# Two halves of the activations in one product: a block product per bank in the up projection of a decoder block

## What is computed

```python
up = rmsnorm(h, g_ffn) @ w_up                  # 512 x 2048 @ 2048 x 11264
up = causal_depthwise_conv(up, conv_w, conv_b) # width 3
gate, val = jnp.split(up, 2, axis=-1)
h = h + (jax.nn.silu(gate) * val) @ w_down     # 512 x 5632 @ 5632 x 2048
```

## Time and profile before

| | us |
|---|---|
| median of 3 runs | 2804.92 (2804.79 to 2805.13) |
| the profiled execution, its own time | 2804.52 |
| its span in the trace | 2803.0 |
| busy in the span: TensorE, its weight loads | 2796.8, 2512.3 |
| busy in the span: VectorE, ScalarE, POOL | 2086.9, 1249.5, 428.8 |

### The profile page before, as it was taken

How to read it: one execution, slowest core, us unless ns; L and a number is a source line. 1 busy time by engine, 2 the same in 40 slices (tenths; PEclk the granted TensorE clock), 3 DMA queues, 4 the chain that set the end, 5 groups by cost and what they waited for, 6 DMA issues and landing times.

```text
span 2803.0 us, 45334 instructions
## 1 busy us (share of the span) xinstructions
PE 2796.8 (100%) x16930; PEld 2512.3 (90%) x16930; DVE 2086.9 (74%) x3913; ACT 1249.5 (45%) x1701; POOL 428.8 (15%) x579
## 2 busy tenths in 40 slices
PE   9999999999999999999999999999999999999999
PEld 7888888888889998888899999999999999999998
DVE  7776777677678777444468987888788878887884
ACT  5444343443434334333355544444444444444543
POOL 2022144323400000000000111111011101010112
PEclk9999999999999999999999999999999999999999
DMA  5464586665535555444455665566656555565567
GB/s 181 142 177 103 170 203 133 170 189 119 120 111 161 174 167 175 149 134 147 139 175 141 144 139 136 133 138 136 136 136 136 136 136 136 136 137 138 135 136 166
DMA packets 187463, 411.24 MB, mean 147 GB/s; under 512 B 22288, under 2 KB 50320, under 8 KB 186128
## 3 DMA queue, kind: packets, MB, share of 16 engines
q1 hardware_dynamic: 120240, 283.90, 32.5%
q0 software_dynamic: 67040, 124.82, 24.2%
HBM read 347.81 MB, written 112.72 MB: 164 GB/s over the span
## 4 chain that ended last, share of the span: by engine, by line
PE 98%; DVE 1%; ACT 0%; issue 0%; DMA 0%; SPq 0%; DVEq 0%
PE bank L1881 12%; PE bank L1883 12%; PE bank L1882 12%; PE bank L2151 11%; PE bank L2153 11%; PE bank L2152 11%; PE bank L2186 6%; PE bank L2187 6%; PE bank L2188 6%; PE bank L2107 3%; PE bank L2109 3%; PE bank L2108 3%; PE bank L1955 1%; PE bank L1989 1%; PE bank L2000 0%; PE bank L1945 0%
## 5 line engine op out<-in xcount | busy, mean ns | idle before, releaser
L2151 PE MATMUL bank<-v_hi,w_hi 128*128 128x256 f32 x2464 | 697.6, 283 | 0.0
L2153 PE MATMUL bank<-v_hi,w_lo 128*128 128x256 f32 x2464 | 697.3, 283 | 0.0
L2152 PE MATMUL bank<-v_lo,w_hi 128*128 128x256 f32 x2464 | 697.3, 283 | 0.0
L937 ACT ACTIVATE w_hi<-w_raw 128x896 fp32r<-128x896 f32 (+1 forms) x528 | 445.2, 846 | 552.1 <-DVE w_raw L1677 384.5
L1684 DVE TENSOR_TENSOR w_lo<-w_raw,w_hi 128x896 fp32r<-128x896 f32 (+1 forms) x528 | 500.0, 953 | 124.5 <-ACT w_hi L937 123.5
L2151 PEld LDWEIGHTS bank<-v_hi,w_hi 128*128 128x128 f32 x2464 | 472.9, 192 | 2.0 <-issue 0.2
L2152 PEld LDWEIGHTS bank<-v_lo,w_hi 128*128 128x128 f32 x2464 | 472.9, 192 | 1.9 <-issue 0.2
L2153 PEld LDWEIGHTS bank<-v_hi,w_lo 128*128 128x128 f32 x2464 | 472.9, 192 | 0.0
L1881 PE MATMUL bank<-u_hi,w_hi 128*128 128x512 f32 x1000 | 395.4, 395 | 0.2 <-DVE w_lo L1078 0.2
L1883 PE MATMUL bank<-u_hi,w_lo 128*128 128x512 f32 x1000 | 389.9, 390 | 0.0
L1882 PE MATMUL bank<-u_lo,w_hi 128*128 128x512 f32 x1000 | 389.3, 389 | 0.0
(11 more groups left out here) (290 smaller groups left out, 4848.7 us busy)
## 6 DMA issues: line engine op xcount, KB each, us to landing
w_raw<-wslots SPq DMA_DIRECT2D x504, 256.0 KB, 2.7
w_raw<-wstream SPq DMA_DIRECT2D x189, 512.0 KB, 3.6
out_t<-stage POOLq DMA_DIRECT2D x168, 256.0 KB, 4.4
sums_scratch<-wfirst POOLq DMA_DIRECT2D x72, 448.0 KB, 5.8
g_raw<-sums_scratch SPq DMA_DIRECT2D x48, 448.0 KB, 3.3
g_raw<-wgates SPq DMA_DIRECT2D x48, 256.0 KB, 2.8
w_raw<-sums_scratch SPq DMA_DIRECT2D x24, 448.0 KB, 3.3
sums_scratch<-sums_scratch POOLq DMA_DIRECT2D x72, 128.0 KB, 4.6
```

What stands on the lines that cost most here:

```text
L937: act.activation(w4_hi[ring][:, 0:width], w4_raw[ring][:, 0:width], ACT.Copy).then_inc(w4_hi_ready, 1)
L2151: nc.tensor.matmul(out, wh, xh, start=kp == 0 and half == 0, stop=False, skip_group_check=True)
L2152: nc.tensor.matmul(out, wh, xl_, start=False, stop=False, skip_group_check=True)
L2153: ins = nc.tensor.matmul(out, wl, xh, start=False, stop=kp == KP - 1, skip_group_check=True)
```

## The change

For the tiles f = 7 to 43 (`WIDE` = 7) the up slots are computed in another way.

- The high and the low activations of a place lie in one tensor, `v_parts`. High weights times high activations (256 columns) and high weights times low activations (256 columns) become one matmul of 512 columns. It fills a whole bank: the left half with the first, the right half with the second. Low weights times high activations is added to the left half. A slot is 7 matmuls of 512 and 7 of 256 columns.
- The 7 block products take banks 0 to 6. The down outputs of a tile go to banks 7, 0, 1, 7 (d0 to d0 + 3); those behind the last tile go to banks 2 to 5.
- In a slot all high weights come first, behind a wait for the high part alone, and then the low ones, behind a wait for the low part. In the last slot, kp = 7, banks 0 to 2 come first with both parts (`EARLY` = 3), then banks 3 to 6. Down slots also take their high weights first.
- At q = 8 ScalarE copies the right halves of the banks (`low_halves`), three together ahead of its `hi_slot` and four together behind it, in place of the half bank of `p1_copy`; VectorE adds the left halves to them (`add_halves`), in two more instructions, the first ahead of its `sums` and `lo_slot`, the second at the head of `combine`. `bank_free` stands on TensorE ahead of each bank's first product of a tile. `combine_wide` and `take_up_wide` do the same five steps as before, from SBUF.
- `take_down(d0 + 2)` moves from q = 2 of the next tile to q = 11, behind `hi_slot(n + 3)`; `take_down(d0 + 3)` moves from q = 4 to q = 2.

```diff
+WIDE_PRODUCTS = [(A11, B11), (S2, T2), (S3, T3), (A22, T4), (S1, T1), (A12, B21), (S4, B22)]
...
+    def down_bank(d):
+        if d >= END:
+            return bank[2 + d % GROUP]
+        return bank[(7, 0, 1, 7)[d % GROUP] if wide(d // GROUP + 2) else GROUP + d % GROUP]
...
+            def low_halves(f, late):
+                if late:
+                    act.wait_ge(slot_done, START_F[f] + KP)
+                    act.wait_ge(s_raw_ready, f)
+                    act.activation(part_list(late_sum, 4), bank_halves(EARLY, 7, 1),
+                                   ACT.Copy).then_inc(low_copied, 1)
+                else:
+                    act.wait_ge(early_done, f - WIDE + 1)
+                    act.wait_ge(up_out, f - 1)
+                    act.activation(part_list(early_sum, EARLY), bank_halves(0, EARLY, 1),
+                                   ACT.Copy).then_inc(low_copied, 1)
...
-                if f > 2 and q in (2, 4):
+                if 2 < f < WIDE and q in (2, 4):
                     take_down(n, d0 - 2 + (q == 4), slots_done)
+                if f >= WIDE and q == 2:
+                    take_down(n, d0 - 1, slots_done)
...
                     if q == KP + 2:
                         conv_term(n, f, 0)
                         take_down(n, d0 + 1, slots_done)
                     if q == KP + 3:
+                        take_down(n, d0 + 2, slots_done)
                         conv_term(n, f, 1)
...
+            def add_halves(f, late):
+                k = 2 * (f - WIDE) + late
+                sums, j0, j1 = (late_sum, EARLY, 7) if late else (early_sum, 0, EARLY)
+                dve.wait_ge(low_copied, k + 1)
+                dve.tensor_tensor(part_list(sums, j1 - j0), bank_halves(j0, j1, 0), part_list(sums, j1 - j0),
+                                  ALU.add).then_inc(drained, 1)
...
+            def bank_free(f, j):
+                d = GROUP * (f - 3)
+                if f == WIDE:
+                    if j >= GROUP:
+                        pe.wait_ge(down_out, GROUP + d + j - GROUP + 1)
+                    return
+                pe.wait_ge(drained, 2 * (f - WIDE) - (j < EARLY))
+                if j < 2:
+                    pe.wait_ge(down_out, GROUP + d + j + 2)
...
+            def wide_high(f, kp, ring, j):
+                w, x = WIDE_PRODUCTS[j]
+                both = v_parts[kp][:, :].rearrange("p (a c) -> p a c", a=2)[:, :, x * HALF:(x + 1) * HALF]
+                if kp == 0:
+                    bank_free(f, j)
+                nc.tensor.matmul(bank[j].rearrange("p (a c) -> p a c", a=2), w4_hi[ring][:, w * P:(w + 1) * P], both,
+                                 start=kp == 0, stop=False, skip_group_check=True)
```

More of the change, by code:

```diff
@@ L281, in build_program @@
     ntri, nones, nmask = (sb(n, P, tile[j]) for j, n in enumerate(("ntri", "nones", "nmask")))
-    bank = [nc.alloc_psum_tensor(f"bank{j}", [P, SEQ], F32) for j in range(8)]
+    banks = nc.alloc_psum_tensor("bank", [P, 8 * SEQ], F32)
+    bank = [banks[:, j * SEQ:(j + 1) * SEQ] for j in range(8)]
     Z = bank[2:6]
@@ L1008, in position @@
                 slots_done = place(n)[0]
+                if wide(f) and q == KP:
+                    low_halves(f, False)
+                hi_slot(n + 3)
                 d0 = GROUP * (f - 2)
@@ L1045, in position @@
                     if q == KP:
-                        p1_copy(n, f)
+                        if wide(f):
+                            low_halves(f, True)
+                        else:
+                            p1_copy(n, f)
                     if q == KP + 1:
@@ L1706, in _, with combine_wide @@
             lo_slot(1)
+            def add_halves(f, late):
[4 more added lines that the diff above has]
+                                  ALU.add).then_inc(drained, 1)
+            def combine_wide(f):
+                k, done = 2 * (f - WIDE), f * DVE_STEPS4
+                dve.wait_ge(drained, k + 1)
+                dve.tensor_tensor(part(early_sum, 1), part(early_sum, 1), part(early_sum, 0),
+                                  ALU.subtract).then_inc(dve4_step, 1)
+                dve.wait_ge(dve4_step, done + 1)
+                dve.tensor_tensor(part(early_sum, 2), part(early_sum, 1), part(early_sum, 2),
+                                  ALU.subtract).then_inc(dve4_step, 1)
+                dve.wait_ge(drained, k + 2)
+                dve.scalar_tensor_tensor(out=part(early_sum, 3), in0=part(late_sum, 1), scalar=-1.0,
+                                         in1=part(early_sum, 1), op0=ALU.mult, op1=ALU.subtract).then_inc(dve4_step, 1)
@@ new lines, in take_up_wide @@
+            def take_up_wide(f):
+                done = f * DVE_STEPS4
+                dve.wait_ge(dve4_step, done + 2)
+                dve.tensor_tensor(a_pad[1][:, PAD:PAD + SEQ].rearrange("p (a c) -> p a c", a=2),
+                                  part(early_sum, 2).unsqueeze(1).broadcast_to((P, 2, HALF)),
+                                  part_list(late_sum, 2), ALU.add).then_inc(dve4_step, 1)
+                dve.wait_ge(dve4_step, done + 3)
+                first_last = early_sum[:, :].rearrange("p (b c) -> p b c", c=HALF)[:, 0:4:3, :]
+                dve.tensor_tensor(a_pad[0][:, PAD:PAD + SEQ].rearrange("p (a c) -> p a c", a=2),
+                                  late_sum[:, 2 * HALF:4 * HALF].rearrange("p (a c) -> p a c", a=2),
+                                  first_last, ALU.add).then_inc(up_out, 1)
@@ L1722, in take_up @@
             def take_up(n, f):
+                if wide(f):
+                    take_up_wide(f)
+                    return
                 fn = f
@@ L1776, in position @@
             def position(n):
-                sums(n + 3)
-                lo_slot(n + 2)
                 at_ = n
@@ L1782, in position @@
                 q = at_ - START_F[f]
+                if wide(f) and q == KP:
+                    add_halves(f, False)
+                sums(n + 3)
+                lo_slot(n + 2)
                 if at_ == 0:
@@ L2134, in _, with wide_low, wide_products, down_free @@
                 unit3(KP - 1, p, p % 2, p // 2)
+            def bank_free(f, j):
[3 more added lines that the diff above has]
+                        pe.wait_ge(down_out, GROUP + d + j - GROUP + 1)
+                    return
+                pe.wait_ge(drained, 2 * (f - WIDE) - (j < EARLY))
[8 more added lines that the diff above has]
+                                 start=kp == 0, stop=False, skip_group_check=True)
+            def wide_low(kp, ring, j):
+                w, x = WIDE_PRODUCTS[j]
+                return nc.tensor.matmul(bank[j][:, 0:HALF], w4_lo[ring][:, w * P:(w + 1) * P], part(v_hi[kp], x),
+                                        start=False, stop=kp == KP - 1, skip_group_check=True)
+            def wide_products(at_, f, kp, ring):
+                for j0, j1 in ((0, EARLY), (EARLY, 7)) if kp == KP - 1 else ((0, 7),):
+                    for j in range(j0, j1):
+                        wide_high(f, kp, ring, j)
+                    if j0 == 0:
+                        pe.wait_ge(w4_ready, at_ + 1)
+                    for j in range(j0, j1):
+                        ins = wide_low(kp, ring, j)
+                    if j1 == EARLY:
+                        ins.then_inc(early_done, 1)
+                return ins
+            def down_free(d):
+                f, i = d // GROUP + 2, d % GROUP
+                if not wide(f):
+                    pe.wait_ge(down_out, d + 1)
+                elif d >= END + GROUP:
+                    pe.wait_ge(down_out, d + 1)
+                elif d >= END:
+                    pe.wait_ge(drained, 2 * (FT - WIDE))
+                elif i == 0:
+                    pe.wait_ge(down_out, GROUP + d)
+                elif i == 3:
+                    pe.wait_ge(down_out, GROUP + d - 2)
+                else:
+                    pe.wait_ge(drained, 2 * (f - WIDE) + 1)
             def up_slot(n):
@@ L2145, in up_slot @@
                     pe.wait_ge(up_out, (f - 1))
+                if wide(f):
+                    pe.wait_ge(w4_hi_ready, at_ + 1)
+                    wide_products(at_, f, kp, ring).then_inc(slot_done, 1)
+                    return
                 pe.wait_ge(w4_ready, at_ + 1)
@@ L2174, in down_slot @@
                 pe.wait_ge(first_out, 1)
-                pe.wait_ge(w4_ready, at_ + 1)
+                pe.wait_ge(w4_hi_ready, at_ + 1)
                 for c, d, fs, first, last in entry(n)[1]:
                     pe.wait_ge(s_ready, fs[-1] + 1)
-                    pe.wait_ge(down_out, d + 1)
+                    down_free(d)
                     if d == DOWNS[-1][0]:
+                        pe.wait_ge(w4_ready, at_ + 1)
                         ins = in_halves(ring, kk, fs, first)
                         continue
[L2182 to L2189, removed]
+                    out = down_bank(d)[:, :]
+                    for k, f in enumerate(fs, kk):
+                        wh = w4_hi[ring][:, k * P:(k + 1) * P]
```

(7 more changed lines are left out.)

53 lines of the change are left out of this document (32 added, 21 removed).

## The result

The changed kernel takes 2827.17 us (2827.16 to 2827.26), the one before 2804.98 in the runs beside it: the ratio is 1.0079, 95% interval 1.0067 to 1.0091, slower by 22.2 us. The forecast was 2818.0, slower by 13.1, in a range of 2802 to 2834.

A forecast was written before the change was run, and what follows sets the result against it. TensorE's own instructions were taken to set the time. A saving of 27 us, 38.5 us of stalls at 36 boundaries and 1.6 us in the last tile summed to +13.1 us: 2818.0 us, in a range of 2802 to 2834.

The forecast's parts named there:

- its own case: The forecast itself: a stall of 0.87 to 1.3 us a boundary, 2811 to 2826 us; chance 0.64.
- TensorE's saving: Up slots: 7 wide matmuls replace 14 narrow, saving 0.091 us a slot, 0.73 a tile, 27 us in all.
- The stall: TensorE waits for bank 1 at each of 36 tile boundaries: 1.07 us each, bounds 0.9 and 1.5, 38.5 us in all.
- The late copy: ScalarE's copy at a tile's end has 1024 elements, not 256: 0.969 us, later by 0.585.
- In the last tile: The fourth down slot waits for bank 7, which holds d0: 1.6 us, once.
- VectorE's first sums of the next tile: Late copy and late addition shift VectorE's chain by 1.72 us: these sums start at +3.47 instead of +1.75.
- The early part: Copy and addition for banks 0 to 2 end before +0.9, needed at +2.73: hidden, costing nothing.
- The transfer as a second lock: `take_down(d0 + 2)` also waits for d0's transfer, until +11.22 to +11.43, as late as ScalarE; 0.06 us added a boundary.
- rival C: Transfers decide: d0's comes 0.5 us later, stall 1.5 us, 2833.5 us; chance 0.12.
- A: Faster: bank 1 is free in time, the 1.72 us shift swallowed, no boundary stalls, 2778 us; chance 0.10.
- B: About the same: five VectorE chain steps cheaper from SBUF, some 0.3 us together, stall 0.75, 2806.5 us; chance 0.10.
- D: The wide product's moving operand in two runs, 7168 bytes apart, loses the 27 us saving: 2845 us; chance 0.04.

The follow-up runs named there:

- e1: Changed kernel with ScalarE taking d0 + 2 out of bank 1 ahead of the high part of up slot 2, not behind it: 2810.61 us.
- e3: Changed kernel with ScalarE taking d0 + 2 ahead of the high part of up slot 2, into a third stage (early_sum): 2785.22 us.
- e4: Changed kernel with only TensorE's order edited: in a wide tile's first slot banks 2 to 6 come first, banks 0 and 1 last: 2785.44 us.
- e9: Changed kernel with the first slot's products in bank order 0, 2, 3, 1, 4, 5, 6, so bank 1 is wanted two products later: 2810.43 us.
- e5: e4's kernel with each wide product again two matmuls of 256 columns, into the two halves of the same bank: 2809.00 us.
- e6: e4's kernel with high and low activations of a block side by side, so the moving operand is one run of 512: 2785.29 us.

## Why the prediction was right, and by how much it was not

The direction, the place and the mechanism were right; e1, e3, e4 and e9 show each that TensorE loses 36 times the time between wanting bank 1 and getting it. The size was less good: 22.2 us were measured for 13.1, within the range, but 1 us above the 2811 to 2826 that the prediction gave to its own case. Three terms of the sum were off.

- **TensorE's saving**: forecast 27 us (0.73 a tile). Measured 20.15 - 19.55 = 0.60 a tile, 22 us. The rate of the wide product was an average over the 48 of the down stage, most of which come behind their like. In the changed kernel seven follow on seven narrow ones, and take 2212.67 - 2211.06 = 1.61 us, 0.230 each. The kernel before has exactly that price in its trace, 1.62 us for the first seven behind a narrow one; the prediction saw it as a slow start in the average and corrected the wrong way, from 0.088 to 0.091 us a slot, where it was the very place that the new products would have. A slot is 19.55 / 8 = 2.44 us and not the 2.43 of the sum (2.444 and 2.427). That makes 5 us.
- **The stall**: forecast 1.07, measured 31.63 - 30.47 = 1.16 us, a tile less one of e4. The late copy took 1.03 and not 0.97, and TensorE started 0.14 behind the copy's end, where the earlier trace rows had shown 0.05. 36 x 0.09 = 3 us.
- **POOL's late issue** in one tile: 0.6 us, not in the sum. The trace of the kernel before had it, in the same tile.

13.1 + 5 + 3 + 0.6 = 21.7 of the 22.2 us. In the last tile TensorE waited for 1.4 us, about as forecast. All three misses point the same way; twice as large, they would have carried the time out of the range, which ends at +29.

Point by point: VectorE's first sums of the next tile started at +3.53, forecast +3.47. VectorE was busy for 10.62 + 16.79 = 27.4 us of the tile, forecast at most 27.7, and didn't become the bound. The early part hid, as no wait names it. The transfer as a second lock was there (e1, e3), but it opened 0.6 us ahead of ScalarE and not beside it: the turnaround of 4.92 and 5.13 us had been read off two transfers of the last tile, and in the others it is near 4.5 (e1). Why those two took longer isn't shown. Here are POOL's issues of d0 and of d0 + 2 in the changed kernel:

```profile
2202.92 0.85 POOL L662 DMA_DIRECT2D out_t<-stage  x1 [17.50 <-ACT stage L1031]
...
2208.90 0.85 POOL L662 DMA_DIRECT2D out_t<-stage  x1 [0.87 <-ACT stage L1031]
```

With the issue at +6.37 the stage was free at about +10.9, and ScalarE came at +11.48. The 0.06 us added for it were for nothing, and of rival C, slower because transfers decide, only the one late tile came true. The upper bound of 1.06 for the late copy can't be had from the earlier trace rows, which give 1.07 to 1.08; with 1.03 measured it changed nothing.

Of the rivals: A (the shift is swallowed) falls with the chain above, in which VectorE has no gap. B (five VectorE steps cheaper from SBUF) falls too: the steps of `take_up` have 0.60 us each in the chain, from SBUF, and their form of 512 had 0.684 us as duration before and has 0.68 now, so the table of the Trainium skill in "VectorE: DVE Perf Modes" (its section on the TRN2 errata), by which a step from PSUM would be an estimated 65 ns dearer than one from SBUF, is again not what this trace shows. D (the two runs eat up the saving) falls with e5 and e6. By the fixed 2.5 ns that the Trainium skill gives in "TensorE: Matmul & The Clock Gate", section "Wait — 56ns, not 53.3ns?", e5 would have been an estimated 5 us slower than e4; it was 23.6.

## What to carry to other kernels

When two uses share a buffer that each had for itself, write down the date on which it comes free and the date on which it is wanted, through every engine's fixed order; the difference, times the number of times, is the price, and it can exceed what the change saves on the busiest engine. Here the cheapest cure was to ask for the contested buffer last: a new order of seven products was worth 42 us and cost no instruction. And price an instruction by rows in which its neighbours are those it will have, not by an average over a stage.

## What was not expected of the hardware

- The first seven matmuls of 512 columns behind narrow ones start 0.231 us apart and later ones 0.2267; wide and narrow in turn cost 4.5 ns a pair more than seven and seven. Which part of TensorE this is, no run here tells.
- A product whose moving operand is two runs of 256 columns, 7168 bytes apart, costs the same as one run: 2785.44 and 2785.29 us.
- POOL issued one transfer 1.3 us late, in the same tile in every run and with nothing in the trace that it waited for, and in the changed kernel that tile took 0.6 us more.
